# Where the first tile's dots begin: second recurrence, second mixing and last projection chunks against the 128 steps of the first period

## What is computed

```python
h = x + concat([diff_attention_heads, hgrn2_heads], -1) @ w_out   # both from rmsnorm(x) @ w_in
y = rmsnorm(h + peer(rmsnorm(h)))

def block(xb):                                    # peer, 128 rows, 8 heads
    qh = (xb @ w_q).reshape(128, 8, 2, 64)
    s = einsum('thcd,hcnd->thcn', qh, sub_keys)   # 128 keys in each half
    s1, i1 = top_k(s[:, :, 0], 16); s2, i2 = top_k(s[:, :, 1], 16)
    top_s, sel = top_k(s1[..., :, None] + s2[..., None, :], 16)
    eidx = chosen(i1 * 128 + i2, sel)             # 16 of 16384 experts a head
    act = gelu(einsum('td,thkd->thk', xb, u_tab[eidx]))
    return einsum('thk,thkd->td', softmax(top_s) * act, v_tab[eidx])
```

## Time and profile before

| | us |
|---|---|
| median of 3 runs | 4038.03 |
| lowest, highest | 4016.13, 4046.87 |
| the profiled execution | 4012.75 |
| its span, first to last instruction | 4010.1 |
| TensorE busy in it (matmul) | 2782.6 (69%) |
| VectorE busy | 2534.7 (63%) |
| GpSimd busy | 2264.1 (56%) |
| ScalarE busy | 1055.4 (26%) |
| mean rate of the DMAs | 346 GB/s |

### The profile page before, as it was taken

How to read it: one execution, slowest core, us unless ns; L and a number is a source line. 1 busy time by engine, 2 the same in 40 slices (tenths; PEclk the granted TensorE clock), 3 DMA queues, 4 the chain that set the end, 5 groups by cost and what they waited for, 6 DMA issues and landing times.

```text
span 4010.1 us, 48464 instructions
## 1 busy us (share of the span) xinstructions
PE 2782.6 (69%) x16300; PEld 1408.8 (35%) x16300; DVE 2534.7 (63%) x6869; ACT 1055.4 (26%) x2881; POOL 2264.1 (56%) x2372
## 2 busy tenths in 40 slices
PE   7999999578578757784777478758874674333365
PEld 6845644343234324442443143224342321000011
DVE  2445757775877687768776787688667556544400
ACT  3312212322232223232332333233322111111021
POOL 1102443666666666666666666666656666666665
PEclk9999999768677857786778587768875675555577
DMA  7645798999999999999999999999999999999998
GB/s 206 199 133 166 264 342 266 381 375 389 367 371 373 400 377 365 375 389 365 360 384 377 369 370 379 385 378 365 375 375 362 379 393 352 365 377 366 368 364 314
DMA packets 544179, 1389.40 MB, mean 346 GB/s; under 512 B 59752, under 2 KB 223680, under 8 KB 543936
## 3 DMA queue, kind: packets, MB, share of 16 engines
q0 software_dynamic: 335136, 1215.01, 80.2%
q1 hardware_dynamic: 198288, 161.34, 12.6%
q10 hardware_dynamic: 10512, 9.97, 0.8%
HBM read 1352.93 MB, written 33.04 MB: 346 GB/s over the span
## 4 chain that ended last, share of the span: by engine, by line
DVE 15%; PE 14%; DMA 14%; POOL 11%; issue 9%; another core or an unknown queue 8%; ACT 2%; DVEq 0%; ACTq 0%; POOLq 0%
DMA d_ub<-in_peer_u_dram,d_eid 7%; DMA d_vb<-in_peer_v_dram,d_eidT 7%; DVE d_ub L1931 6%; POOL d_vb L1737 5%; POOL d_ub L1718 5%; PE d_pY L1767 4%; PE r_pB L1467 2%; PE d_pS L866 2%; PE d_pS L952 1%; PE d_pS L932 1%; PE d_pS L891 1%; PE d_pS L880 0%; DVE t_shared_ids L1133 0%; PE r_pB L1657 0%
## 5 line engine op out<-in xcount | busy, mean ns | idle before, releaser
L1931 DVE CUSTOM_DVE_ANT_0 d_ub<-d_ub,d_pX 128x1024 f32<-128x1024 f32 x1024 | 1242.3, 1218 | 641.6 <-DMA d_ub<-in_peer_u_dram,d_eid 523.2
L1718 POOL DMA_INDIRECT d_ub<-in_peer_u_dram,d_eid x1152 | 1134.9, 985 | 876.8 <-DVE d_hdot L1931 395.4
L1767 PE MATMUL d_pY<-d_vb,d_dg 128*32 128x256 f32 x8768 | 954.7, 516 | 856.2 <-DMA d_vb<-in_peer_v_dram,d_eidT 577.3
L1737 POOL DMA_INDIRECT d_vb<-in_peer_v_dram,d_eidT x1096 | 1042.3, 951 | 731.0 <-issue 258.7
L1767 PEld LDWEIGHTS d_pY<-d_vb,d_dg 128*32 128x32 f32 x8768 | 256.5, 128 | 1461.9 <-issue 1281.3
L1806 ACT ACTIVATE d_dg<-c_late_sb,d_wgtT 128x32 f32<-128x32 f32 x1152 | 334.3, 314 | 1228.8 <-PE d_pY L1767 745.1
L718 PE MATMUL d_pX<-d_wq,d_vb 128*128 128x512 f32 (+3 forms) x1536 | 473.5, 461 | 19.8 <-ACT d_xs L579 12.0
L718 PEld LDWEIGHTS d_pX<-d_wq,d_vb 128*128 128x128 f32 x1536 | 270.4, 199 | 185.5 <-issue 116.4
L1931 DVE CUSTOM_DVE_ANT_0 d_ub<-d_ub,d_vb 128x1024 f32<-128x1024 f32 x128 | 155.5, 1223 | 48.7 <-DMA d_ub<-in_peer_u_dram,d_eid 47.0
L1467 PEld LDWEIGHTS r_pB<-r_side,c_small_sb 128*128 128x128 f32 x1152 | 177.3, 245 | 22.9 <-issue 13.3
L1467 PE MATMUL r_pB<-r_side,c_small_sb 128*128 128x128 f32 (+15 forms) x1152 | 177.6, 324 | 11.0 <-DVE r_side L1396 6.7
(11 more groups left out here) (289 smaller groups left out, 3561.1 us busy)
## 6 DMA issues: line engine op xcount, KB each, us to landing
d_vb<-in_w_in_dram SPq DMA_DIRECT2D x68, 512.0 KB
d_ub<-in_peer_u_dram,d_eid POOLq DMA_INDIRECT x1152
d_vb<-in_peer_v_dram,d_eidT POOLq DMA_INDIRECT x1096
r_side<-in_cache_k_dram SPq DMA_DIRECT2D x16, 1024.0 KB
r_side<-in_cache_v_dram SPq DMA_DIRECT2D x16, 1024.0 KB
d_wo<-in_w_out_dram SPq DMA_DIRECT2D x6, 2048.0 KB, 8.2
d_wo<-in_peer_w_q_dram SPq DMA_DIRECT2D x4, 2048.0 KB, 8.7
scratch_h<-t_shared SPq DMA_DIRECT2D x9, 512.0 KB
```

The lines of the kernel that those rows point to most:

```text
L1718: pool.indirect_dma_start(out=ub[:, g % R, :], out_offset=None, in_=io["peer_u"][0], in_offset=off).then_inc(u_in[g % R], 16)
L1737: pool.indirect_dma_start(out=to, out_offset=None, in_=io["peer_v"][0], in_offset=off).then_inc(landed, 16)
L1767: m = nc.tensor.matmul(pY[q * QT:(q + 1) * QT, g % 2, :], dg[:, n % DG, :], rows[:, q * QD:(q + 1) * QD], start=k % QT == 0, stop=k % QT = ...
L1931: nc.vector.tensor_tensor_reduce(out=ub[:, g % R, :], in0=ub[:, g % R, :], in1=xflat if i else xn_of(0), scale=1.0, scalar=0.0, op0=ALU.mu ...
```

## The change

A function maps positions. Those below -47 move by 45 steps, so that the first tile's turned ids come two steps ahead of step 0. Those from -47 on are pressed linearly: -47 becomes -2, 0 becomes 32.9, and 128 becomes 128. It is applied to all projection chunks and norms, to mixing 0 and 1 and to recurrence 0 and 1. The recurrences from the third on (position 118 in this period) and the mixings from the third on keep their positions. Steps, dots, gathers and `FIRST` are unchanged, and so is every instruction.

```diff
@@ -204,6 +204,11 @@
     pos += [78 + 4.4 * n for n in range(10)]
 
+    def early(s):
+        return s + 45 if s < -47 else (s + 47) * 130 / 175 - 2
+
+    pos = [early(s) for s in pos]
+
     def segments_of(n):
@@ -409,7 +414,7 @@
-        norm_at = [-300, pos[4] + 0.8] + [pos[12 + 2 * i] + 1.5 for i in range(6)] + [-118]
+        norm_at = [early(-300), pos[4] + 0.8] + [pos[12 + 2 * i] + 1.5 for i in range(6)] + [early(-118)]
@@ -673,7 +678,7 @@
                 if i == NT - 1:
-                    yield -161.5
+                    yield early(-161.5)
@@ -778,7 +783,9 @@
         def local(i, at):
-            return NEXP * (i - 1) + FIT[i] * at if i else at - 162
+            if i < 2:
+                return early(FIT[1] * at if i else at - 162)
+            return NEXP * (i - 1) + FIT[i] * at
@@ -1224,7 +1231,7 @@
         def when(r, at):
-            return recur_at[r] + at
+            return recur_at[r] + at if r > 1 else early(recur_at[r] + at)
```

## The result

The changed kernel took 4049.13 us as a median of 10 runs (4037.93 to 4062.15), the kernel before 4029.24 us in the 10 runs beside them. The ratio is 1.0042 with a 95% interval of [1.0027, 1.0057]: some 17 us (11 to 23) slower, inside 1%. The forecast said 4041 us and +3 us, with bounds of -9 and +21 on the difference: the side and the bounds are right, the size of +3 is not. The profiled execution took 4047.28 us with a span of 4044.3 us.

A forecast was written before the change was run, and what follows sets the result against it. TensorE was taken as the bound from 318.9 to 697.1 us, gathers (DMA) from 721.6. Terms +17 - 3 - 11 = +3 us on the 4038.03 us median gave 4041 us; forecast 4029 to 4059, stated range 4010 to 4080.

The forecast's parts named there:

- Nothing moves ahead of the ids, TensorE is the bound up to 697.1 us, the rest follows the second tile's start: Whole run: no cost before the first ids, TensorE bound from 318.9 us, everything from 721.6 us shifted with that start.
- Start of the dots: First tile: the first dot moves from 361.3 to about 318.9 us, 42.4 us, the most that could be gained.
- rival 3: Claimed the dots were the bound, so all 42.4 us come back: 3996 us; chance 0.07.
- The second recurrence behind dots: After the turned ids: dots ahead in VectorE's queue delay the recurrence and TensorE's stream by 17 us, bounds 9 and 27.
- rival 2: At 319 to 400 us, gathers and TensorE's lower clock make it slower: 4080 us; chance 0.12.
- The clock: At the second recurrence: matmuls behind longer waits run at the lower level, making the sum 2 to 5 us higher.
- TensorE's slack behind it: The 336 us of TensorE's work behind the second recurrence: VectorE is relieved, 3 us gained, bounds 0 and 6.
- Tail: Around 697.1 to 721.6 us: the third recurrence's sigmoid comes one chunk earlier, gaining 11 us, bounds 6 and 12.
- carried along one for one: From the second tile's first dot at 721.6 us: any shift of that start moves the rest equally.

The follow-up runs named there:

- e1: The kernel before with VectorE's queue order of the changed kernel, all other queues as before; ratio to the kernel before 1.0040 [1.0020, 1.0059].
- e9: The changed kernel with the 47 units from ahead of the first dot given 16 dots' room, the other 128 the rest; ratio to the kernel before 1.0005.
- e2: The changed kernel with VectorE's queue order of the kernel before, all other queues as changed; ratio to the kernel before 0.9983 [0.9965, 1.0001].
- e5: The kernel before with its last two projection chunks 3.8 steps later and the end 2.7; ratio to the kernel before 0.9998 [0.9986, 1.0010].
- e7: The kernel before with its last two projection chunks later and the 4 MB query weight load cut to an eighth; ratio to the kernel before 0.9951.
- e12: The changed kernel with the 4 MB query weight load cut to an eighth; ratio to the kernel before 1.0022 [1.0007, 1.0036].

## Why the prediction was right, and where it was not

- *Nothing moves ahead of the ids, TensorE is the bound up to 697.1 us, the rest follows the second tile's start.* Right. A and B of the profile of after add up to +19.3 us, against +17 (11 to 23) in the runs; e1 gives 15.3 against 16 (8 to 24).
- *Start of the dots.* Right: 322.14 us, and no gain from it; rival 3 is out, since e9 has the same early dots and takes the time of before.
- *The second recurrence behind dots, +17 us (9 to 27).* The mechanism is right: e1 and e2 show it. The size was too small: TensorE came to head 1's spread 30.8 us late, 23.3 of waits and 7.4 at the lower clock, and that is outside the bounds. Head 1's pairs were ready 80.0 us behind the ids (402.26 - 322.22), where I had 66.7. Two steps were mis-sized. The first is the pace: I took 1.85 us a dot from four slots and the median landing, and the trace shows 2.12, so the recurrence began 5 us later than I had it. The DMA share of this stretch, which I had held against rival 2 as 0.30, became 0.81 once the gathers were in it. The second is the way from head 0's pairs to head 1's, 26.6 us in place of 19.3: I had TensorE's spread, half segment and state matmuls at the higher clock there, some 7 us, and they took 13.2 (375.70 to 388.9), for which VectorE stood 5.16 us; one gather wait of 2.7 us came on top. The first wait grew to 19.8, I had named 15.
- *The clock.* I had left it out of the sum and named 2 to 5 us as what it might add. It added 7.4 us up to head 1's spread, of which 3.2 came back behind it. The Trainium skill (TensorE: Matmul & The Clock Gate, Part 1: The HAM clock gate) says that the array's clock is throttled by default and that activity releases it. The trace agrees: behind a wait of 5.91 us a spread took 7.00 us at a granted clock of 0.50, and the same matmuls without a wait ahead of them 3.63.
- *TensorE's slack behind it, -3 us (0 to 6).* Right in sign, and outside its bounds, too: -11.0 us. Idle time fell by 7.8 us (9.9 to 2.2; among it the wait of 3.7 us at L922) and the clock gave 3.2.
- *Tail, -11 us, carried along one for one.* The first half is right: 10.0 us at the second tile's first dot, by the sigmoid as described. "Carried along one for one" is the step that failed. I had followed the path to the first dot only and had not asked what the DMA engines do at that moment. The 4 MB load stands in their queue there, issued at 724.60 us and landed 23 us later, and each step of the second tile wants two gathers of 512 KB. B is 68.3 us in place of 68.8; e5 shows the same without the rest of the change, e7 and e12 show the gain arriving when the load is cut.
- The sum: +30.8 - 11.0 - 10.0 = +10 at the second tile's first dot, counted from the ids (13.1 us in the trace, 3.3 of them from ahead of the ids), against +3 with bounds of -9 and +21; then +9.5 for the tail given back, +19. That +19 lies inside the bounds is luck in part: the first two terms were each outside their own bounds, in opposite directions, and the third was wrong in kind.
- *Rival 2* was nearer in the first part than my forecast: it had TensorE's stream 40 us late there, by gathers and clock together, and it was 30.8. Its point of decision, four dots in 9.6 us, was nearly reached (8.5 for the first 14). Where it went wrong is that late weight chunks would eat the gains of the other two terms: 11.0 us came back up to the projections' end, and the tail's gain was lost to the load of the query weights.

## What to carry to other kernels

In an engine's queue count, for each piece that another engine waits for, what stands ahead of it, priced by the slowest feed of those instructions (here a gather's round, 2.1 us, not the 1.14 us of the dot), and add what the waiting engine's next instructions take at the lower clock; moving a piece forward only moves the wait on, unless each slot holds as much work of the waiting engine as its own instruction takes. When work is pressed into fewer slots, spread it by the time of the bound engine and not by the number of steps. A gain at the head of a DMA-bound stretch counts only if no large load is issued there: follow it some transfers further, and look at the DMA share with and without it.

## What the runs showed of the hardware

- Chips differ by more than any of these changes: the kernel before took 4004, 4004 and 4031 us on three chips and 3825 us on a fourth. The DMA-bound part shows it, 395 GB/s against 373, while A of the same order, 395.7 us, is close to that of the slower chip, 398.3. The first 14 dots took 28.4 us there, against 29.7 in after and 28.6 in e1, so at this place the gathers' pace hardly differs between the chips.
- A gather's round is not its bytes alone: with a quarter of them the pace went from 2.12 to 1.66 us a dot. The Trainium skill (DMA: Bandwidth & Descriptors, Anatomy of one DMA) gives a fit for one DMA, a fixed part of 2.0 us and 436 GB/s; by it a gather of 512 KB would be an estimated 3.2 us. The trace doesn't agree for gathers that share the engines: the first of after, issued at 323.63 us, let its dot start at 328.62 (5.0 us), and the median of before was 5.9 us.
- The stretch ahead of the ids, in which nothing differed between these kernels, ended anywhere between 312.3 and 326.7 us in the profiled executions. Whoever compares two traces has to begin behind it.
